# The V sums of the 16 meta rows move from TensorE to VectorE, and their gathers into four ring groups

## What is computed

```
def one_block(hb):                      # a block of tokens, normed
    ...                                 # 8 heads, 16 best of 128 x 128 experts each
    u = expert_u[idx]                   # 128 rows of 1024 for each token
    act = gelu(einsum('tnd,td->tn', u, hb))
    return einsum('tn,tnd->td', gate * act, expert_v[idx])
h = h + peer_ffn(h, ...)                # added to the residual
```

## Time and profile before

| | |
|---|---|
| median of 3 runs | 3090.97 us (3090.78 to 3094.11) |
| the profiled execution's own time | 3100.33 us |
| its span, first to last instruction | 3098.5 us |
| mean granted clock of PE | 0.935 |

### The profile page before, as it was taken

One profiled execution on the slowest core, in us unless ns is written; L12 is line 12 of the kernel. 1 busy time (PEld: TensorE's weight loads), 2 busy tenths in 40 slices (PEclk: granted clock), 3 DMA queues, 4 the chain that ended last, 5 costly groups with the idle time before them and its releaser, 6 DMA issues.

```text
span 3098.5 us, 27338 instructions
## 1 busy us (share of the span) xinstructions
PE 2660.9 (86%) x6968; PEld 1235.1 (40%) x6968; DVE 2090.6 (67%) x6393; ACT 583.1 (19%) x1773; POOL 997.6 (32%) x1107
## 2 busy tenths in 40 slices
PE   7999999898898788867988888888898889887777
PEld 3675444343343333423433434343344334333333
DVE  1124459788688758766778668875877588755555
ACT  1126112111111111111111211121112111111111
POOL 0000133333333333323333333333333333333332
PEclk9999999999999999989998999999998999889999
DMA  3221169999999999999999999999999999999997
GB/s 110 82 109 75 57 263 419 392 393 422 421 421 418 399 415 421 419 414 420 400 418 415 416 397 421 421 412 403 419 415 410 411 418 407 417 418 419 417 417 313
DMA packets 166341, 1134.89 MB, mean 366 GB/s; under 512 B 21136, under 2 KB 22160, under 8 KB 30768
## 3 DMA queue, kind: packets, MB, share of 16 engines
q0 software_dynamic: 149760, 1090.59, 85.7%
q1 hardware_dynamic: 16432, 42.62, 3.7%
HBM read 1130.97 MB, written 2.10 MB: 366 GB/s over the span
## 4 chain that ended last, share of the span: by engine, by line
DMA 46%; PE 36%; DVE 11%; issue 6%; ACT 1%; SPq 0%; POOL 0%; POOLq 0%; ACTq 0%; DVEq 0%
DMA ring_early<-in_peer_vu,idx_u 17%; PE psum L1404 17%; DMA ring_early<-in_peer_uv,idx_u 16%; DMA ring_late<-in_peer_uv,idx_u 7%; PE psum L1023 6%; DMA ring_late<-in_peer_vu,idx_u 5%; DVE ring_early L1498 3%; PE psum L681 3%; PE psum L585 3%; PE psum L721 2%; PE psum L617 2%; DVE ring_late L1498 1%; DVE work L1140 1%; DVE si L1138 1%; PE psum L1418 1%
## 5 line engine op out<-in xcount | busy, mean ns | idle before, releaser
L1404 PE MATMUL psum<-ring_early,w_col 128*128 128x512 f32 x2784 | 1352.0, 629 | 231.1 <-ACT w_col L1451 214.5
L1498 DVE SCALAR_TENSOR_TENSOR ring_early<-ring_early,psum 128x1024 f32<-128x1024 f32 x696 | 846.8, 1217 | 433.8 <-DMA ring_early<-in_peer_uv,idx_u 219.6
L1404 PEld LDWEIGHTS psum<-ring_early,w_col 128*128 128x128 f32 x2784 | 551.5, 202 | 948.2 <-issue 820.8
L1404 PE MATMUL psum<-ring_late,w_col 128*128 128x512 f32 x1376 | 668.5, 625 | 103.0 <-ACT w_col L1451 96.0
L1498 DVE SCALAR_TENSOR_TENSOR ring_late<-ring_late,psum 128x1024 f32<-128x1024 f32 x344 | 418.6, 1217 | 209.0 <-DMA ring_late<-in_peer_uv,idx_u 137.5
L1385 POOL DMA_INDIRECT ring_early<-in_peer_vu,idx_u x348 | 329.7, 947 | 617.2 <-DVE ring_early L1498 264.5
L1385 POOL DMA_INDIRECT ring_early<-in_peer_uv,idx_u x348 | 328.0, 943 | 584.5 <-DVE ring_early L1498 265.5
L1451 ACT ACTIVATE w_col<-ident,weight 128x128 f32<-128x128 f32 x1024 | 343.3, 392 | 641.3 <-DVE weight L1480 637.0
L1404 PEld LDWEIGHTS psum<-ring_late,w_col 128*128 128x128 f32 x1376 | 270.1, 201 | 453.7 <-issue 395.9
L1445 ACT ACTIVATE ge<-ga 128x4 f32<-128x4 f32 x260 | 53.3, 205 | 1368.9 <-DVE ga L1466 1368.9
L1023 PE MATMUL psum<-wq,hbT 128*128 128x512 f32 x512 | 272.3, 619 | 18.4 <-DVE work L1140 17.2
(11 more groups left out here) (223 smaller groups left out, 1732.6 us busy)
## 6 DMA issues: line engine op xcount, KB each, us to landing
wq<-in_peer_w_query SPq DMA_DIRECT2D x16, 1024.0 KB, 18.3
w_ring<-in_even_w_in SPq DMA_DIRECT2D x6, 2048.0 KB, 8.2
ring_early<-in_peer_vu,idx_u POOLq DMA_INDIRECT x348, 12.8
ring_early<-in_peer_uv,idx_u POOLq DMA_INDIRECT x348, 12.8
w_ring<-in_even_w_out SPq DMA_DIRECT2D x1, 4096.0 KB, 14.1
ring_late<-in_peer_vu,idx_u POOLq DMA_INDIRECT x172, 12.8
ring_late<-in_peer_uv,idx_u POOLq DMA_INDIRECT x172, 12.8
hres<-in_x SPq DMA_DIRECT2D x4, 512.0 KB, 4.9
```

What stands on the lines that cost most here:

```text
L1404: ins = nc.tensor.matmul(y_ps[:, half, :], w_col[:, i % W_SLOTS, :], v_cell(at)[:, 512 * half:512 * half + 512], start=False, stop=i == CH ...
L1498: nc.vector.scalar_tensor_tensor(out=cell, in0=cell, scalar=1.0, in1=rows, op0=ALU.mult, op1=ALU.mult, accum_out=dot[par][:, i:i + 1]).the ...
```

## The change

The V sums of rows 0 to 15 leave PE. DVE adds each row's v, times the row's weight of each partition, in place to hres[:, 4, :] (add_meta_vector), whose lower 112 partitions a new load fills with zeros; the meta tokens' residual is in the upper 16. add_meta_vector for row k stands in DVE's list behind the dot (and the weights step, if there is one) of row k + 6, so the last six stand in tile(0). When all 16 are added, PE folds the tile once with the matrix fold (fold_meta_tensor), between its routing steps of the meta chunk and tile(0), and ACT copies the fold's 16 partitions back as before. ACT makes no w_col for meta rows any more. All 16 meta rows go to groups 0 to 3 in turn, in one call of gather_pool; late_constants with its wait for the projections comes behind them, then bands; tile(0)'s rows begin with group 4. The gather of a row waits for s_madd where it waited for the PE sum of a meta row. PE's query steps of the meta chunk run with nothing between them.

More of the change, by code:

```diff
@@ L71 @@
 RING = GROUPS_EARLY + GROUPS_LATE
-META_ORDER = [0, 1, 2, 3, 0, 1, 2, 3, 4, 5, 0, 1, 2, 3, 4, 5]
-EARLY_ROWS = META_ORDER.index(GROUPS_EARLY)
-assert len(META_ORDER) == CHUNK and META_ORDER[-1] == RING - 1
-ORDER = META_ORDER + [n % RING for n in range(2 * XT * TILE_ROWS)]
+META_ORDER = [n % GROUPS_EARLY for n in range(CHUNK)]
+ORDER = META_ORDER + [(n + GROUPS_EARLY) % RING for n in range(2 * XT * TILE_ROWS)]
 class Place:
@@ L87, in __init__ @@
         self.dotted = before[-1] + 1 if self.uses > 0 else None
-        self.summed = before[-2] + 1 if self.uses > 1 else None
+        self.summed = before[-2] if self.uses > 1 else None
 def first_piece(job):
@@ L337, in program @@
         s_acc = sem("slot_summed")
+        s_madd = sem("meta_row_added")
+        s_msum = sem("meta_rows_folded")
+        s_mzero = sem("rows_below_meta_zeroed")
         s_yadd = sem("tile_added")
@@ L1398, in sums_tensor @@
             for i in range(CHUNK):
-                at = Place(j, i if j is None else CHUNK * c + i)
-                n = CHUNK * u + i
+                at = Place(j, CHUNK * c + i)
+                n = CHUNK * (u - 1) + i
                 pe.wait_ge(s_ring[at.group], 16 * (at.uses + 1))
@@ L1405, in sums_tensor @@
                                            v_cell(at)[:, 512 * half:512 * half + 512],
-                                           start=False, stop=i == CHUNK - 1 and (j is None or c == TILE_CHUNKS - 1),
+                                           start=False, stop=i == CHUNK - 1 and c == TILE_CHUNKS - 1,
                                            skip_group_check=True)
@@ L1411, in open_sum @@
         def open_sum(pe, j):
-            rows = META_ROWS if j is None else tile_of(j % XT)
-            n = META if j is None else P
+            rows = tile_of(j % XT)
             for half in range(2):
-                if j is not None:
-                    pe.wait_ge(s_yadd, 2 * j + 1 + half)
-                nc.tensor.matmul(y_ps[:, half, :], ident[0:n, :], rows[:, 512 * half:512 * half + 512],
+                pe.wait_ge(s_yadd, 2 * j + 1 + half)
+                nc.tensor.matmul(y_ps[:, half, :], ident[:, :], rows[:, 512 * half:512 * half + 512],
                                  start=True, stop=False, skip_group_check=True)
+        def add_meta_vector(dve, i):
[15 more added lines that the diff above has]
+            last.then_inc(s_msum, 1)
         def take_scalar(act, j):
@@ L1433, in stage_u, with columns_scalar @@
             nc.scalar.copy(idx_u[par][:, :], idxT[:, cols(u)]).then_inc(s_idx_u, 1)
-        def columns_scalar(act, j, c, base, hooks=()):
+        def columns_scalar(act, j, c, hooks=()):
             u = number(j, c)
@@ L1447, in columns_scalar @@
                 if j is not None:
[L1448 to L1452, removed]
+                    n = CHUNK * (u - 1) + i
+                    if n >= W_SLOTS:
+                        act.wait_ge(s_acc, n + 1 - W_SLOTS)
+                    nc.scalar.activation(w_col[:, i % W_SLOTS, :], ident[:, :], ACT.Copy,
+                                         scale=weight[par][:, i:i + 1]).then_inc(s_wcol, 1)
                 at_token(hooks, i)
@@ L1478, in gelu_weights @@
             dve.wait_ge(s_gmul, m + 1)
-            wait(dve, s_wcol, QUAD * (m - 2 * QUADS + 1))
+            if m >= 3 * QUADS:
+                dve.wait_ge(s_wcol, QUAD * (m - 3 * QUADS + 1))
             nc.vector.tensor_tensor(weight[par][:, x], gx[:, :], ge[:, :], ALU.mult).then_inc(s_weight, 1)
@@ L1680, in tile @@
                         stage = [(0, next_indices)]
-                    columns_scalar(act, j, c, ident, stage + of_chunk(hooks, c))
+                    columns_scalar(act, j, c, stage + of_chunk(hooks, c))
             def kept(j):
@@ L1690, in _ @@
             early = routing_scalar(act, 1, META_QUERIED, 2)
-            columns_scalar(act, None, 0, fold, of_chunk(early, 0) + [(12, lambda: piece_exponentials(act, 1))])
+            columns_scalar(act, None, 0, of_chunk(early, 0) + [(12, lambda: piece_exponentials(act, 1))])
             tile(0, [(at - CHUNK, f) for at, f in early if at >= CHUNK] +
@@ L1834 @@
     inputs["peer_vu"] = np.concatenate([inputs["peer_v"], inputs["peer_u"]], axis=2)
+    meta = inputs["meta_tokens"]
+    inputs["meta_tokens"] = np.concatenate([meta, np.zeros((P - META, D), meta.dtype)])
     for name in _INS:
```

## The result

The changed kernel takes 3123.32 us in the median of six runs (3118.65 to 3130.95), the kernel before 3093.75 in six; the ratio is 1.0087, 95% interval 1.0072 to 1.0102. It is slower by 29.6 us, inside the range given, 6 us above the number given.

A forecast was written before the change was run, and what follows sets the result against it. The prediction took DMA's row queue, full from about 428 us, as the bound; 22.1 us for row 16's later landing, 3.7 for the hole and 1.0 at the start made 26.8, so 3117 us, range 3102 to 3129.

The forecast's parts named there:

- Row 8 comes 6.4 us later: Row 8's gather waits for DVE's addition of row 0, behind row 6's dot: issued at 429.6 us, 6.4 later.
- Rounds of 9.4 and 8.8 us for a pair: Gathers of rows 8 to 15 alternate with DVE's additions, at most two on their way: 9.4 or 8.8 us a pair.
- Bands uncovered, 7.0 us: Bands on POOL, now behind row 15, no longer hides behind queued gathers: 7.0 us, row 16 issued at 470.0.
- PE late, a hole of 3.7 us: PE starts tile(0) late behind addition 15 and a slow fold; row 28, issued at 504, leaves DMA idle 3.7 us.
- The start, 1.0 us: At kernel start, loading the zeros ahead of w_in and the small loads delays DVE and PE: 1.0 us.
- What is taken off gives nothing: The removed PE matmuls and ACT columns, at 424 to 466 us beside a full DMA, bring no gain.
- Rival A: In tile(0), additions make DVE the bound, 2.8 us a row against DMA's 2.5: 8 us more, 3126; chance 0.10.
- Rival B: The late start is hidden because something other than DMA sets the pace later: no difference, 3091 to 3097; chance 0.06.
- Rival C: Rows 8 to 12 move in DMA's idle 410 to 423 us if the first exponential starts before 407: 3078.5; chance 0.05.
- Rival D: DVE's additions hold POOL's gathers 8 to 15 through SBUF contention: 10 us more, 3127; chance 0.07.

The follow-up runs named there:

- fold_aside: early_exp with the fold moved behind the sum of tile(0)'s seventh row and only 8 useless matmul records before open_sum; 3095.0 us, 0.9998 of the kernel before.
- early_exp: all_fixes with ACT's first exponential moved from behind projection 9 to behind projection 7; 3091.4 us, 0.9988 of the kernel before.
- bands_late: The changed kernel with bands behind the gathers of tile(0)'s first two chunks instead of behind row 15; 3123.4 us, 1.0088 of the kernel before.
- pe_warm: The changed kernel with four useless matmul records released by each of additions 10 to 15, before the fold; 3122.8 us, 1.0096 of the kernel before.
- all_fixes: The changed kernel with additions four rows behind, bands behind the second chunk, zeros behind w_out, PE kept at work before the fold; 3110.5 us, 1.0045 of before.

## Why the prediction was right, and where its sizes were off

Its direction, mechanism and range held; the two sizes it gave to the first rows came out nearly to the tenth, the two behind them were small.

- *Row 8 comes 6.4 us later.* Right: 7.4 us behind the last projection's copy against 1.1, 6.2 us later. An addition takes 1.28 us.
- *Rounds of 9.4 and 8.8 us for a pair.* Right: rows 8, 10, 12 and 14 are issued at 421.84, 431.16, 440.01 and 449.60, rounds of 9.3, 8.9 and 9.6; row 15 follows by 3.5 us where 3.7 was given.
- *Bands uncovered, 7.0 us.* Right in place, 1.5 us short: from 454.95 to 463.44, 8.5 us. The prediction kept 0 to 2.6 us for it in the range and took 0. Row 16's gather moved by 23.7 us where 22.7 follows from its 470.0, its landing by 23.3 where it gave 22.1.
- *PE late, a hole of 3.7 us.* The step that was mis-sized (by its own times the hole comes to 4.0). Row 28's gather came at 83.7 us behind DVE's resumption; the prediction's 504 is 81.2. The difference lies in front of the fold: addition 15 ended at 71.9 where 69.5 was given, half of it from row 16's later landing, while the way from there to row 28's gather took 11.8 us against 11.7. With it came what the prediction left out: row 28 is followed by one gather every 2.6 us, and meanwhile DMA isn't full. The share is 0.64 at 490 to 500 and 0.91 at 500 to 510 us, and from row 16's landing to row 31's the loss is 6.3 us, not 3.7. The bytes of the windows say the same, as an estimate: 80 us behind the copy DMA has moved 23.9 MB against 34.0 before, 24 us' worth at 420 GB/s, and 100 us behind it 29.8 against 42.4, 30 us' worth.
- *The start, 1.0 us.* Wrong in its parts and harmless: 2.2 us at DVE, 0.6 at PE.
- *What is taken off gives nothing.* Right: 46 us of PE work less and no gain.

The sum by these measurements is 23.3 + 6.3 + 0.6 = 30.2 us against 29.6 in the medians and 31.9 in the rest. That the prediction's 26.8 came out short of all three, with its mechanism right, is the sizes of bands and of the hole. Rival A, DVE as the bound of tile(0), was not seen in the change, where DVE waits 2.69 us for row 28 at 504.70. What holds fold_aside is DVE too, but earlier and in another way than rival A had it: DVE works without a wait from 412.51 us to the stage behind row 23's dot, and PE's next product waits for it to have read the scores. Rival B fell: nothing was hidden later. Rival C was priced and conditioned rightly as far as its place goes, and early_exp met the condition. Rival D holds only for bands.

What stays open: why bands_late and pe_warm gain 8.0 and 7.5 us in one execution's rest, 8.5 and 5.9 in the lag, and next to nothing in the medians of five. The mixer scatters by 10 us over the profiles and the time behind row 60 by 5.6, which may be enough for it, but that was not tested; what each of the two steps costs is thus known only from traces. The records of no use in all_fixes and early_exp were never taken out with all else left in place. Nor was a kernel tried in which DVE's top-k stages stand elsewhere, which the hole in fold_aside points to.

## What to carry to other kernels

When DMA bounds a kernel, look for the moment from which its queue never runs dry, and count the transfers that may be on their way before it. A release that comes from the same in-order engine that waits for the landings makes a round trip of each; where the release stands in that engine's list (here four or six rows behind) was worth more than the work, 12.6 against 4.3 us in the medians. Work that is hidden has its cover on a certain line: a step moved past the gathers that covered it stands in the gathers' way for its full length. A filler that keeps an engine at work is itself work in that engine's list: give it an end that comes before what it is to speed up. And where single runs scatter, count from an event that the change can't touch.

## What had not been expected of the hardware

Bands' instructions that read SBUF were held by additions in two places: the select at 456.51 took 1.33 us against 0.29 for its like and ended 0.14 us behind the addition of 456.42 to 457.70, and four selects at 459.42 took 2.09 together against 1.09 before, beside the addition at 459.83. The gathers' instructions took 0.94 to 1.40 us up to 498 us, so rival D's 1.3 us for each of the eight is not there. The Trainium skill, SBUF — State Buffer, section Who interferes with whom, says just this of a DVE instruction with two SBUF inputs and a GpSimd instruction that reads SBUF; the traces agree, and with bands moved away (bands_late, 541.93 us) the four selects take 1.03 us again.
